# Choosing the sample's experts for four heads at once, one head on each group of 32 partitions

## The reference

```python
def chunk(xc):
    q = (xc @ w_pq).reshape(c, PEER_HEADS, 2, PEER_HALF)        # 8 heads, 2 x 128
    s = jnp.einsum('chpd,hpkd->chpk', q, sub_keys)              # 128 keys per half
    sv, si = lax.top_k(s, PEER_TOPK)                            # 16 of 128, twice
    cand = (sv[:, :, 0, :, None] + sv[:, :, 1, None, :]).reshape(c, PEER_HEADS, -1)
    cid = (si[:, :, 0, :, None] * PEER_NKEYS + si[:, :, 1, None, :]).reshape(c, PEER_HEADS, -1)
    cv, ci = lax.top_k(cand, PEER_TOPK)                         # 16 of 256
    eid = jnp.take_along_axis(cid, ci, axis=-1)
    gate = jax.nn.softmax(cv, axis=-1)
    act = jax.nn.gelu(jnp.einsum('chkd,cd->chk', u_emb[eid], xc), approximate=False)
    return jnp.einsum('chk,chkd->cd', gate * act, v_emb[eid])
```

## Time and profile before

| | |
|---|---|
| time, median of 3 runs | 1046.88 us (1045.89 to 1047.12) |
| profiled execution, its span | 1044.4 us |
| busy: PE, DVE, ACT, POOL | 768.4, 761.5, 410.3, 617.4 us |
| DMA, all queues | 381.40 MB, mean 365 GB/s |
| software queue (the gathers) | 304.81 MB, 75.3% of 16 engines' span |
| hardware queue (SyncE's loads) | 75.71 MB, 19.7% |

### The profile page before, as it was taken

The page is one execution under the profiler, slowest core; times in us unless marked ns, Lnnn a source line. Parts: engine busy times, 40 slices in busy tenths (PEclk is TensorE's granted clock), DMA queues, the critical chain, the costliest instruction groups (busy, mean ns, idle before and its releaser), DMA issues.

```text
span 1044.4 us, 13759 instructions
## 1 busy us (share of the span) xinstructions
PE 768.4 (74%) x4077; PEld 379.5 (36%) x4077; DVE 761.5 (73%) x1927; ACT 410.3 (39%) x1159; POOL 617.4 (59%) x584
## 2 busy tenths in 40 slices
PE   8999996456978869777559766765875855645966
PEld 3575872112544546444113333331322422211211
DVE  1362858998877454999977699999554598999441
ACT  1153133223754752333324453732774323324221
POOL 0000257777777776666676757557475665777771
PEclk9999998886987989998767968987687888886899
DMA  9924699999999999999999999999899999999994
GB/s 363 317 106 178 219 331 399 410 404 345 369 397 400 351 410 404 415 407 376 374 375 382 394 406 389 366 392 394 310 407 419 415 415 411 409 402 343 408 410 186
DMA packets 122109, 381.40 MB, mean 365 GB/s; under 512 B 15915, under 2 KB 40315, under 8 KB 116787
## 3 DMA queue, kind: packets, MB, share of 16 engines
q0 software_dynamic: 83696, 304.81, 75.3%
q1 hardware_dynamic: 38338, 75.71, 19.7%
HBM read 378.03 MB, written 4.14 MB: 366 GB/s over the span
## 4 chain that ended last, share of the span: by engine, by line
DVE 43%; PE 21%; DMA 15%; POOL 9%; issue 6%; SPq 3%; ACT 3%; ACTq 0%; DVEq 0%; POOLq 0%
PE bank L445 13%; DVE rows L1388 10%; DMA rows<-in_peer_u,eid 8%; PE acc L445 6%; POOL rows L1883 4%; DVE ql_t L1683 4%; DVE small L1682 4%; DMA w_uq_sb<-in_w_uq 3%; POOL rows L1901 3%; DMA rows<-in_peer_v,eid 2%; DVE more_u L1388 2%; DVE first_u L1388 2%; DVE shared L1714 2%; DVE shared L1725 2%; DMA z<-in_cache_kv 2%
## 5 line engine op out<-in xcount | busy, mean ns | idle before, releaser
L445 PE MATMUL acc<-rows,spread 128*64 128x512 f32 (+1 forms) x1024 | 356.7, 719 | 117.0 <-DMA rows<-in_peer_v,eid 95.2
L1883 POOL DMA_INDIRECT rows<-in_peer_v,eid x256 | 271.2, 1060 | 130.6 <-issue 69.0
L1901 POOL DMA_INDIRECT rows<-in_peer_u,eid x184 | 199.0, 1082 | 99.4 <-issue 48.2
L445 PEld LDWEIGHTS acc<-rows,spread 128*64 128x64 f32 (+1 forms) x1024 | 92.0, 156 | 308.7 <-issue 270.7
L1388 DVE CUSTOM_DVE_ANT_0 rows<-rows,xr_even 128x1024 f32<-128x1024 f32 x89 | 108.3, 1219 | 48.5 <-DMA rows<-in_peer_u,eid 47.6
L1388 DVE CUSTOM_DVE_ANT_0 rows<-rows,xr_odd 128x1024 f32<-128x1024 f32 x95 | 116.1, 1222 | 31.8 <-DMA rows<-in_peer_u,eid 31.1
L1901 POOL DMA_INDIRECT first_u<-in_peer_u,eid x37 | 39.6, 1069 | 96.8 <-DVE eid L1775 79.2
L1056 ACT ACTIVATE spread<-wide_consts,wts 128x64 f32<-128x64 f32 (+1 forms) x288 | 83.7, 337 | 15.5 <-PE acc L445 11.0
L445 PE MATMUL acc<-more_v,spread 128*64 128x512 f32 (+1 forms) x128 | 71.2, 681 | 22.2 <-DMA rows<-in_peer_v,eid 21.3
L1047 ACT ACTIVATE gelus<-dots 128x2 f32<-128x2 f32 x144 | 28.8, 200 | 130.5 <-DVE dots L1388 129.8
L1049 ACT ACTIVATE wts<-gelus,gate 128x1 f32<-128x1 f32 x288 | 69.1, 287 | 4.7
(11 more groups left out here) (267 smaller groups left out, 1336.8 us busy)
## 6 DMA issues: line engine op xcount, KB each, us to landing
wring<-in_w_pq SPq DMA_DIRECT2D x12, 1024.0 KB, 8.0
rows<-in_w_pq SPq DMA_DIRECT2D x3, 2048.0 KB, 8.5
z<-in_w_pq SPq DMA_DIRECT2D x5, 1024.0 KB, 8.0
wring<-in_cache_ckv SPq DMA_DIRECT2D x40, 128.0 KB, 7.0
rows<-in_w_in SPq DMA_DIRECT2D x2, 2048.0 KB, 15.0
rows<-in_peer_v,eid POOLq DMA_INDIRECT x256, 9.6
wring<-in_w_out SPq DMA_DIRECT2D x4, 1024.0 KB, 11.6
wring<-in_cache_kv SPq DMA_DIRECT2D x32, 128.0 KB
```

Source lines behind the costliest of these rows:

```text
L445: return T.matmul(o, lhsT=l, rhs=r, start=start, stop=stop, skip_group_check=True)
L1883: nc.gpsimd.indirect_dma_start(out=v_ring[n % RV], out_offset=None, in_=inp["peer_v"], in_offset=bass.IndirectOffsetOnAxis(ap=eid[t][:, n ...
L1901: nc.gpsimd.indirect_dma_start(out=u_ring[U_PLACE[n]], out_offset=None, in_=inp["peer_u"], in_offset=bass.IndirectOffsetOnAxis(ap=eid[t][: ...
```

## The change

The query projection keeps its four columns. The scores of two columns now go into one bank: the four heads of a *quad*, each on its own 32 partitions, with only two sets of 128 scores beside each other on a partition. VectorE's steps of choosing run once for a quad, after columns 1 and 3, on 128 partitions with one head in the free direction, and not after each column. Expert numbers and gates are written directly to `eid[2]` and `gate[2]`: a slot of the sample is now one rank of four heads. A quad opens 16 slots (256 and 272). The weights of `share` add up to the same; the four pauses of a quad issue `share(2 * CHOOSE)` each, and after columns 0 and 2 none is issued. ScalarE's exponential is done for a quad, and its `queries` waits for `first_pair_scored` where before it waited for a full bank.

```diff
-PARTS = [[(0, 1), (1, 1), (2, 2), (4, 2), (6, 2)]] + [[(2 * c, 2) for c in range(4)]] * 2
+PARTS = [[(0, 1), (1, 1), (2, 2), (4, 2), (6, 2)], [(2 * c, 2) for c in range(4)], [(0, 1), (1, 1)]]
+STARTS = [[16 * h for h, _ in p] for p in PARTS]
 CHOSEN = [sum(len(p) for p in PARTS[:t]) for t in range(3)]
...
                         experts.advance(CHOOSE)
+                if t == 2:
+                    quad = ("sc", c // 2, t)
+                    b = banks[turn[quad] % NRING] if c % 2 else take(pe, quad)
+                    for half in range(2):
+                        for j in range(2):
+                            g = 32 * (2 * (c % 2) + j)
+                            i = mm(b[g:g + 32, half * 128:(half + 1) * 128], qp_t[c % 2][:, 2 * j + half, 0:n],
+                                   keys_t[:, 4 * c + 2 * j + half, :])
+                    if c % 2:
+                        full(i, quad)
+                    else:
+                        i.then_inc(first_pair_scored, 1)
+                    return
                 b = take(pe, ("sc", c, t))
                 for j in range(4):
                     i = mm(b[0:n, j * 128:(j + 1) * 128], qp_t[c % 2][:, j, 0:n], keys_t[:, 4 * c + j, :])
@@ -999,9 +1014,9 @@
                             z_product_of_sample(q)
                     else:
                         query_product(c, t)
-                    if t:
+                    if t == 1 or t == 2 and c % 2:
                         for i in range(4):
-                            share(CHOOSE)
+                            share(CHOOSE * t)
                     elif c == 1:
                         next_tiles_z(2, 0, 8)
                 if t == 0:
...
-                if c > 1:
+                if c > 1 and t == 2:
+                    if c == 2:
+                        act.wait_ge(first_pair_scored, 1)
+                    else:
+                        ready(act, ("sc", 0, t))
+                elif c > 1:
                     ready(act, ("sc", c - 2 if t or c > 2 else "b", t))
                 copy(name, qp_t[c % 2][:, :, 0:P[t]], split(b[:, 0:4 * P[t]], 4, P[t]))
 
@@ -1345,11 +1365,13 @@
                         share(W_PQ)
                         queries(c, t)
                         share(W_PQ)
-                        share(CHOOSE)
-                        share(CHOOSE)
-                        gate_exps(t, c)
-                        share(CHOOSE)
-                        share(CHOOSE)
+                        if t == 2 and c % 2 == 0:
+                            continue
+                        share(CHOOSE * t)
+                        share(CHOOSE * t)
+                        gate_exps(t, c // t)
+                        share(CHOOSE * t)
+                        share(CHOOSE * t)
                     experts.rest(t - 1)
                     if t == 2:
                         y_root(1)
...
                         pause()
-                link(V, V.scalar_tensor_tensor(out=eu[0:n, ks], in0=ea[0:n, ks], scalar=float(KEYS), in1=eb[0:n, ks],
-                                               op0=ALU.mult, op1=ALU.add))
-                spread_slots(t, p, eid[t], eu).then_inc(slots_ready, 1)
+                i = V.scalar_tensor_tensor(out=(eid[2] if t == 2 else eu)[0:n, ks], in0=ea[0:n, ks], scalar=float(KEYS),
+                                           in1=eb[0:n, ks], op0=ALU.mult, op1=ALU.add)
+                if t == 2:
+                    i.then_inc(slots_ready, 1)
+                else:
+                    link(V, i)
+                    spread_slots(t, p, eid[t], eu).then_inc(slots_ready, 1)
                 dve.wait_ge(gate_exp, CHOSEN[t] + p + 1)
                 link(V, V.tensor_reduce(out=small[0:n, 96:96 + m], in_=gt[0:n, hs, :], axis=AX.X, op=ALU.add))
                 link(V, V.reciprocal(small[0:n, 104:104 + m], small[0:n, 96:96 + m]))
                 rc = free(small[0:n, 104:105], (1, m), (0, PTOP))
-                link(V, V.tensor_tensor(gt[0:n, hs, :], gt[0:n, hs, :], rc, ALU.mult))
-                link(V, spread_slots(t, p, gate[t], gt[:, :, :].rearrange("p h k -> p (h k)")))
+                if t == 2:
+                    link(V, V.tensor_tensor(gate[2][:, ks], gt[:, h0, :], free(small[:, 104:105], (0, PTOP)), ALU.mult))
+                else:
+                    link(V, V.tensor_tensor(gt[0:n, hs, :], gt[0:n, hs, :], rc, ALU.mult))
+                    link(V, spread_slots(t, p, gate[t], gt[:, :, :].rearrange("p h k -> p (h k)")))
                 pause()
 
             def spread_slots(t, p, o, a):
 
-                m, every = (WIDE, PAIR) if t < 2 else (32, 1)
+                m, every = WIDE, PAIR
                 k0, k1 = (16 * h for h in (PARTS[t][p][0], sum(PARTS[t][p])))
                 for j in range(every):
                     for q in range(128 // m):
@@ -1831,7 +1860,12 @@
                 for c in range(4):
                     share(W_PQ)
                     share(W_PQ)
-                    if t:
+                    if t == 2 and c % 2 == 0:
+                        continue
+                    if t == 2:
+                        best_keys(t, c // 2, 1, ("sc", c // 2, t))
+                        choose(t, c // 2, lambda: share(2 * CHOOSE))
+                    elif t == 1:
                         best_keys(t, 2 * c, 2, ("sc", c, t))
                         choose(t, c, lambda: share(CHOOSE))
                     elif c:
...
-                    if j in [h * SLOTS[t] // 8 for h, _ in PARTS[t]]:
-                        pool.wait_ge(slots_ready, CHOSEN[t] + [h * SLOTS[t] // 8 for h, _ in PARTS[t]].index(j) + 1)
+                    if j in STARTS[t]:
+                        pool.wait_ge(slots_ready, CHOSEN[t] + STARTS[t].index(j) + 1)
                     if n in (2, 6):
                         ready(pool, ("pq", {2: 1, 6: 2}[n], 0))
                     if n == U_GUESTS[0][0]:
```

More of the change, by code:

```diff
@@ L359, in build @@
         root_ready = Signal("root_ready", ROOTS)
+        first_pair_scored = sem("first_two_heads_of_a_quad_scored")
         gate_sub = sem("gate_sub")
@@ L1290, in gate_exps @@
                 h, m = PARTS[t][p]
-                g = gt[0:P[t], h:h + m, :]
+                g = gt[:, h:h + m, :]
                 act.wait_ge(gate_sub, CHOSEN[t] + p + 1)
@@ L1728, in best_keys @@
             def best_keys(t, h0, m, name):
-                n, b = P[t], ready(dve, name)
+                n, b = 128, ready(dve, name)
                 top16([b[0:n, j * 128:(j + 1) * 128] for j in range(2 * m)], [sc[0:n, j, :] for j in range(2 * m)],
@@ L1734, in choose @@
             def choose(t, p, pause):
-                n, (h0, m) = P[t], PARTS[t][p]
+                n, (h0, m) = 128, PARTS[t][p]
                 hs = slice(h0, h0 + m)
```

## The result

| | before | after | ratio, 95% interval |
|---|---|---|---|
| first comparison, 5 runs each | 1046.94 us (1045.89 to 1049.67) | 1036.31 us (1035.14 to 1039.39) | 0.992 (0.9903 to 0.9937) |
| second, 29 and 12 runs | 1044.26 us (1037.95 to 1049.84) | 1039.99 us (1035.36 to 1043.87) | 0.9964 (0.9946 to 0.9981) |
| third, 17 and 6 runs | 1044.07 us (1041.06 to 1047.54) | 1038.10 us (1034.08 to 1040.41) | 0.9939 (0.9915 to 0.9963) |

The ratio isn't the quotient of the two medians: in the first row it makes 8.4 us of the change, and the medians make 10.6.

What follows compares the result with a forecast made beforehand. DMA bytes bound the end, except one 30 us dip while VectorE's choosing held up GpSimd's gathers. Filling it gives up to 5.05 us, less 0.5: 1046.88 - 4.5 = 1042.4 us, range 1040.5 to 1046.3.

Steps and rivals of the forecast that it cites:

- The bound: From 900 us to the end DMA bytes bind, except one dip at 940 to 970 us with 349 GB/s.
- VectorE's load: In 834 to 950 us choosing falls from 64.7 to 18.4 us, so VectorE loses 46 us of work.
- The waits: GpSimd's 17.7 us of waits for VectorE's dot products, 830 to 960 us, nearly all go, to under 5.
- What that is worth: Only the bytes missing at 900 to 970 us: 2.7 to 5.05 us, 4.5 chosen after 0.5 off for a store.
- The upper end: 2,070 KB short of full rate at 900 to 970 us, worth 5.05 us at 410 GB/s.
- the two measures of the dip: Gain at 900 to 970 us: 5.05 us by bytes short of full rate, 2.7 us by DMA busy share.
- Does the lead last: GpSimd's slow pace to slot 263 loses 4 us of a 22 us queue, which stays above 15, filling the dip.
- the signs: Expected marks, among them 405 GB/s or more from 900 us and u gathers near 950 us landing in 15 or more.
- Rival A: GpSimd's own slow issue pace, 924 to 952 us, makes the dip: 0.6 us gained, 1046.3 us; chance 18%.
- Rival B: Scores of columns 1 and 3 come no earlier, VectorE idles: 2.5 us slower, 1049.4 us; chance 7%.
- Rival C: Memory gives no more than 349 GB/s in the dip, so no gain: 1046.9 us; chance 3%.
- Handover and tail: After tile 1's last sum TensorE is free some 3 us earlier, unused; the tail moves as a block.

Runs made afterwards that it cites:

- before_half_choice: Kernel before, with the sample's numbers and gates worked out for even heads only and used for odd ones too; 1040.68 us, ratio 0.9973.
- same_after: Kernel after, unchanged, timed again beside the kernel before; 1039.99 us, ratio 0.9964.
- same_after_5: Kernel after, unchanged, once more, in the series of the table's third row; 1038.10 us, ratio 0.9939.
- after_full_load: Kernel after, with 36 useless VectorE instructions in each quad, in four pieces beside the choosing; 1059.37 us, ratio 1.0141.
- same_before_2: Kernel before, unchanged, in a disturbed series; profiled span 1110.2 us.
- same_after_3: Kernel after, unchanged, one of three repeats in disturbed series, whose ratios were 0.9909, 0.9991 and 1.0118.

## Why the prediction was right and wrong

**The bound: right.** Bytes set the end, with one dip. After the change every window from 900 us on is at 406 to 410 GB/s, as the forecast asked.

**VectorE's load: right.** Two quads were to cost 18.4 us; the lines of the choosing, L1733 to L1792, keep VectorE busy 18.1 us. The windows of 834 to 950 us that answer to the earlier trace rows, all of VectorE, the dot products, and the laying out of tile 2's activations (L1420):

```profile
834.00:950.00 116.00, 71.36 (x164) 0.76 1.02 410
...
834.00:950.00 116.00, 48.99 (x82) 0.76 1.02 410
...
834.00:950.00 116.00, 4.89 (x4) 0.76 1.02 410
```

71.36 - 48.99 = 22.4 us aren't dot products, but 4.9 of them are L1420, which before the change falls behind 950 us. So nearly 47 us of choosing went (64.7 - 18.1), where the forecast had 46. Half of it would have given most of the gain.

**The waits: right.** 17.7 to 2.8 us, under the 5 asked for.

**What that is worth: a little small.** The upper end, 5.05 us, was the better term than the 4.5 chosen; 5.4 was measured in the late part, between 4.7 and 6.1. The 0.5 us that I took off for the store and the middle ground between the two measures of the dip had no support: the store of y of tile 1 is issued at 953.45 us in after and at 957.75 in `before_half_choice`, and both have 409 GB/s or more in every 20 us from 940 to 980.

**Does the lead last: right in its end, wrong in its number.** I had the queue above 15 us; the gathers of 900.29 and 933.63 us took 14.34 and 11.70 to land, where the signs asked for 15 or more. The DMA engines were still full, as they are at 1004.11 with 10.23. By these rows a queue of some 10 to 12 us is deep enough.

**Rival A, GpSimd's pace: refuted.** It said that the slow pace makes the dip. In the changed kernel the slow issues are still there and the dip isn't. A gather of GpSimd and the dot product that ran beside it, after:

```profile
910.88 1.98 POOL L1917 DMA_INDIRECT rows<-in_peer_v,eid  x1 [0.30 <-issue]
```
```profile
910.83 1.22 DVE L1410 CUSTOM_DVE_ANT_0 rows<-rows,xr_odd 128x1024 f32<-128x1024 f32 x1
```

Between 820 and 1010 us 70 gathers were issued beside dot products with `xr_even` alone, and none took over 1.05 us; of 29 beside one with `xr_odd` 15 did, up to 1.98. (In `same_after` and `same_after_5` it is 10 of 30 and 10 of 32, again with none beside `xr_even`.) `xr_odd` lies in SBUF like the rows, `xr_even` in PSUM, so these are the instructions with two SBUF inputs, and the Trainium skill's sentence on them (GPSIMD Engine Reference, Specifications) holds here gather by gather. It has a price per gather, up to 1.04 us over the usual 0.94. At the end of the program no price of it shows, since with these issues left the DMA engines stay at 409 GB/s and more.

**Rival B, the pair comes late: refuted as put, and yet the most useful of the three.** The scores came at 841.32 (forecast 845 to 847) and VectorE waited for no bank. But the late start that B feared is real: with the load held up, `after_full_load` was 15 us slower than before, by the late start and the long pieces together. Here VectorE has time left when it starts, and no cost shows.

**Rival C, the memory: refuted** by 410 GB/s in the window of the dip.

**Handover and tail: right, with one omission.** The tail moved as a block, 17.07 and 17.06 us. At the handover I wrote that TensorE's earlier freedom is something "which nothing uses". GpSimd waits there for TensorE, after:

```profile
963.13 0.94 POOL L1917 DMA_INDIRECT rows<-in_peer_v,eid  x1 [4.96 <-PE acc L447]
```

The DMA engines stay at 1.03 beside it, so nothing was lost by it. One more term was off at no cost: the score products were to be the same, and eight of them took 0.63 us (once 1.07) where they took 1.06.

**The step that failed** is the last one, "I subtract the same 4.5 from it: 1046.88 - 4.5 = 1042.4", with a range that gave the runs of before a spread of 0.8 us (the three stood 0.99 below and 0.24 above their median). It took three runs within 1.2 us for the kernel's time. That the median lies 2.5 above the span was no fault: time and span of one execution differ by 1.8 to 2.5 us in all runs. In 46 later undisturbed runs the kernel before took 1037.95 to 1049.84, with medians of 1044.26 and 1044.07, and in its profiles the part that the change doesn't touch differs by 6.3 us. From 1044.2 the same sum gives 1039.7, and the two later comparisons gave 1039.99 and 1038.10. The first comparison's 10.6 us are then 5.4 of change and about 5 of variation: for the two profiled executions this is shown (4.2 of 10.3 us stand ahead of the change); for the other runs of it, which have no profile, it is argued from the medians.

Chance from one execution to the next isn't enough for these 5 us. All five runs of before in the first comparison took 1045.89 or more, as only 7 of the 46 later ones did. The runs of after stood low in it, with a median of 1036.31 that only 2 of its 18 later undisturbed runs reach. So a series differs from the next as a whole; what sets that stays open. The same step made "0.2% (2.1 us) can't be told from none" too sharp: the three undisturbed comparisons of the same two kernels gave 3.8, 6.4 and 8.4 us by their ratios, with intervals that don't all meet.

## What to carry to other kernels

Price a relief by what its bound lacks (here bytes below the full rate in the dip), not by the work removed: 47 us of VectorE's work went, the first half gave most of the gain, and the whole was about the 5 us of missing bytes. Work that is put together in larger groups starts later and in longer pieces; here that was free because the engine had slack, and with the load held it turned 5 us of gain into 15 of loss. When two profiles of a long program are compared, find the last point ahead of the change and subtract there; take the kernel's own spread from repeated series of one and the same program, not from three runs within 1.2 us.

## What the runs showed of the hardware that I had not expected

- One core held 409 to 411 GB/s from HBM for over 150 us (824 to 980 us of after, 411). The Trainium skill has this too, against the sentence that the prediction weighed: Perfetto Trace Analysis, Roofline, puts 358 GB/s as the share of a core when both of a pair access the memory, and says that one active core can pull more. The trace agrees, with 411.
- An execution may fall into a condition in which TensorE and ScalarE stand still 118 and 205 us in all between instructions (`same_before_2`), up to 16.8 us at a time (`same_after_3`), with runs of 1070 to 1112 us; the same chip gave a median of 1044 us at another time.
- TensorE's granted clock falls at other moments from execution to execution of one program. In 556 to 572 us, where TensorE is busy 12.8 to 15.7 of 16 us, a mean of 0.68 goes with 39.6 to 40.6 us for twelve slots and one of 0.89 to 0.91 with 36.2 to 39.1 us; in three of those last four profiles most of the lead was gone eighteen slots later.
- A gather's issue on GpSimd took 0.94 us, and up to 1.98 us beside a VectorE instruction with both inputs in SBUF; beside one with an input in PSUM none of 70 took over 1.05 us.
